# A hybrid decoder step on one core: the decode tail reordered, the output weights loaded inside it, and the gate rows sent through memory

## The reference, cut to what matters

```python
    mod = jax.nn.silu(c) @ lp['w_ada'] + lp['b_ada']
    shift, scale, gate = jnp.split(mod, 3, axis=-1)
    ...
    mixed = jnp.concatenate([jax.nn.silu(mla_gate) * o_mla,
                             jax.nn.silu(rw_gate) * o_rw,
                             jax.nn.silu(gm_gate) * o_gm], axis=-1)
    out = jnp.einsum('ble,ed->bld', mixed, lp['w_out'])
    y = x + gate[:, None] * rms_norm(out, lp['norm_post_g'])
```

## Time and profile before

| | us |
|---|---|
| median of three runs | 1983.21 (1981.27 to 1985.27) |
| the profiled execution | 1974.86 |
| its span, first to last instruction | 1973.3 |
| TensorE busy | 1854.2 |
| DVE busy | 899.1 |
| ACT busy | 514.2 |
| the last block of layer 0 begins | 854.8 |
| the last block of layer 1 begins | 1831.4 |

### The profile page before, as it was taken

How to read it: one execution, slowest core, us unless ns; L and a number is a source line. 1 busy time by engine, 2 the same in 40 slices (tenths; PEclk the granted TensorE clock), 3 DMA queues, 4 the chain that set the end, 5 groups by cost and what they waited for, 6 DMA issues and landing times. The chain is left out here.

```text
span 1973.3 us, 45874 instructions
## 1 busy us (share of the span) xinstructions
PE 1854.2 (94%) x19360; PEld 1160.5 (59%) x19360; DVE 899.1 (46%) x2001; ACT 514.2 (26%) x1186; POOL 181.3 (9%) x175
## 2 busy tenths in 40 slices
PE   3999999999998999989969999999999979998998
PEld 2565676666665666654436656766566646666543
DVE  2124133232585777745230430432318677776542
ACT  3111022222422343411221111222224124343212
POOL 0010000002333100000000200000202340000000
PEclk9999999999999999979989999999999999998899
DMA  9600001000114766353064001010001166662531
GB/s 388 226 11 28 22 22 33 22 11 22 36 54 133 215 195 186 117 215 139 33 238 166 1 27 33 11 33 22 22 23 51 38 183 202 191 191 67 216 139 44
DMA packets 104503, 197.47 MB, mean 100 GB/s; under 512 B 17226, under 2 KB 87324, under 8 KB 100068
## 3 DMA queue, kind: packets, MB, share of 16 engines
q1 hardware_dynamic: 104292, 194.48, 29.8%
HBM read 181.70 MB, written 21.19 MB: 103 GB/s over the span
## 5 line engine op out<-in xcount | busy, mean ns | idle before, releaser
L825 PE MATMUL PB<-RB,R 128*128 128x344 f32 x1632 | 493.2, 455 | 0.0
L825 PEld LDWEIGHTS PB<-RB,R 128*128 128x128 f32 x1632 | 302.0, 190 | 156.4 <-issue 15.2
L2023 PE MATMUL PB<-RB,R 128*128 128x512 f32 x512 | 221.2, 592 | 0.0
L1651 PE MATMUL PB<-WUQ,Q 32*32 32x256 f32 x5120 | 198.8, 385 | 15.8 <-DVE WUQ L1812 9.5
L1812 DVE STREAM_TRANSPOSE WUQ<-RB 128x512 f32<-128x512 f32 x316 | 203.1, 679 | 14.2 <-DMA RB<-in_cache 11.5
L2023 PEld LDWEIGHTS PB<-RB,R 128*128 128x128 f32 x512 | 97.0, 190 | 120.8 <-issue 118.6
L985 ACT ACTIVATE R<-PB 128x344 f32<-128x344 f32 x90 | 41.2, 458 | 401.9 <-PE PB L825 401.9
L1240 DVE TENSOR_TENSOR PB<-PB,CST 128x128 f32<-128x128 f32 x64 | 18.8, 294 | 222.0 <-PE PB L845 222.0
L1651 PEld LDWEIGHTS PB<-WUQ,Q 32*32 32x32 f32 x5120 | 89.4, 104 | 41.3 <-issue 24.6
L673 PE MATMUL PB<-RB,R 128*128 128x344 f32 x288 | 85.4, 459 | 1.8 <-PEq L250 1.8
L1122 DVE COPY R<-PB 128x320 f32<-128x320 f32 x16 | 7.9, 492 | 146.7 <-PE PB L684 146.7
(11 more groups left out here) (368 smaller groups left out, 2658.6 us busy)
## 6 DMA issues: line engine op xcount, KB each, us to landing
RB<-in_cache SPq DMA_DIRECT2D x512, 160.0 KB, 2.6
R<-in_w_in SPq DMA_DIRECT2D x44, 512.0 KB, 3.7
R<-in_w_ada SPq DMA_DIRECT2D x14, 1536.0 KB, 12.5
RB<-in_w_ada SPq DMA_DIRECT2D x6, 1536.0 KB, 13.3
RB<-in_w_out SPq DMA_DIRECT2D x8, 1024.0 KB, 10.4
RB<-out_x_stream SPq DMA_DIRECT2D x2, 4096.0 KB
out_x_stream<-RB SPq DMA_DIRECT2D x16, 512.0 KB
RB<-in_x_prompt SPq DMA_DIRECT2D x1, 4096.0 KB
```

The source lines that it names most:

```text
L825: mm = pe.matmul(jobbank(j)[:, 0:CH], ring[:, blkno[n] % 4, k, :], hT[:, k, chunk(c)], start=(k == 0), stop=(k == KT - 1))
L1651: mm = pe.matmul(PB[qp[o], 2 * (h % 2) + q % 2, 0:256], Q4[qp[q], g, :], k[qp[q], c], start=(g == 0), stop=(g == NB - 1), skip_group_check ...
L2023: mm = pe.matmul(PB[0:n, 2 * (t % 2) + hf, :], mixT[:, k, cols(t)], wo[:, k, hf * 512:(hf + 1) * 512], start=(k == 0), stop=(k == 5))
```

## The change

The w_out loads move into the decode block, behind the last page loads, as their buffers come free; so do the loads of the decode rows and of w_uv. The tail gets a new order with new words: `WP(k)` is tile 0's projection for one k (k=0, 1, 2), and `GT` turns `gp` into rows on TensorE, which ACT copies out and SP writes to memory in four pieces. The last block reads them back, the prompt's row spread over 128 partitions by the DMA. `PV` is now four words of eight records. A square root of one element is put behind GT on ACT. In the last block tile 0's k=3 and half of tile 1 stand between the units of the normalisation, and the load of `ada[1]` joins the three others. The diff, cut:

```diff
+            gp = sm2[:, 80:152].rearrange("p (k c) -> p k c", c=9)
+            wuv2 = R4[:, 2066:3090].rearrange("p (r c) -> p r c", r=2)
+            grows = R4[:, t6 + 624:t6 + 880]
+            gate_rows = a["scr"].rearrange("v b c -> (v b) c")[NS:NS + 36].rearrange("(r g) c -> r g c", g=4)
...
-            TAIL = [(NH - 1, "PT", 0), (NS, "rw", "Z0"), (NH - 1, "PV", 0), (0, "FC", 1), (NS, "rw", "U0"), (0, "FC", 2), (NS, "rw", "H0"),
-                    (NS, "rw", "G0"), (0, "FC", 3), (NS, "rw", "Z1"), (0, "FC", 4), (NS, "rw", "U1"), (0, "FC", 5), (NS, "rw", "H1"),
-                    (0, "FC", 6), (NS, "rw", "OO")]
+            PE_PLAN = PE_PLAN[:-1] + rec("Z0") + PE_PLAN[-1:] + [wp(0)] + rec("U0") + [(NH - 1, "PT", 0)] + rec("H0") + [fc(1), wp(1)] + \
+                rec("Z1") + [fc(2), pv(0)] + rec("U1") + [pv(1)] + rec("H1") + [pv(2), pv(3), fc(4)] + rec("OO") + [wp(2), fc(6), (0, "GT", 0)]
+            ACT_PLAN = ACT_PLAN[:-2] + rec("Z0") + ACT_PLAN[-2:] + rec("U0") + [(NH - 1, "PT", 0)] + rec("Z1") + [fc(3)] + rec("U1", "OO") + [(0, "GT", 0)]
+            DVE_PLAN = pair_plan(DVE_PAIR) + [fc(1)] + rec("H0", "G0") + [fc(2), fc(3), fc(4)] + rec("H1") + [fc(5), fc(6)]
...
                     sp.dma_start(a["scr"][0].rearrange("b (m c) -> (b m) c", c=16), svo).then_inc(sv_io, 16)
+                    sp.wait_ge(sv_io, 16 * 10)
+                    sp.dma_start(orow, a["scr"][0]).then_inc(s_or, 16)
+                    sp.wait_ge(pg_free, 28)
+                    for i in (0, 1):
+                        sp.dma_start(wo[:, 2 * i:2 * i + 2], dram("w_out")[:, 2 * i:2 * i + 2]).then_inc(s_wo[i], 16)
+                    sp.wait_ge(pg_free, 30)
+                    for i in (3, 2):
+                        sp.dma_start(wo[:, 2 * i:2 * i + 2], dram("w_out")[:, 2 * i:2 * i + 2]).then_inc(s_wo[i], 16)
+                    sp.wait_ge(ta_done, NS)
+                    sp.wait_ge(ak_done, NS)
+                    sp.dma_start(wuv2, dram("w_uv")).then_inc(s_uv, 16)
                     sp.wait_ge(st_done, NCH + 1)
                     sp.dma_start(dram("wkv_p"), S0[:, NCH % 4]).then_inc(sv_io, 16)
-                    sp.wait_ge(sv_io, 16 * 11)
+                    sp.wait_ge(gr_done, 1)
+                    for g in range(4):
+                        sp.dma_start(gate_rows[:, g], grows[32 * g:32 * g + 9]).then_inc(sv_io, 16)
+                    sp.wait_ge(sv_io, 16 * 15)
...
+                        elif what == "WP":
+                            pe.wait_ge(xe_done, NH - 1)
+                            pe.wait_ge(s_wo[g // 2], 32)
+                            for hf in range(2):
+                                pe.matmul(PB[:, hf, :], mixT[:, g, 0:P], wo[:, g, hf * 512:(hf + 1) * 512], start=(g == 0), stop=False)
+                        elif what == "GT":
+                            pe.wait_ge(st_done, 1)
+                            pe.wait_ge(ty_done, NS)
+                            for k in range(KT):
+                                mm = pe.matmul(PB[32 * (k // 2):32 * (k // 2) + 9, 5, (k % 2) * P:(k % 2 + 1) * P], gp[:, k, :], ident, start=True, stop=True, skip_group_check=True)
+                            mm.then_inc(gr_full, 1)
...
+                        elif what == "GT":
+                            act.wait_ge(gr_full, 1)
+                            act.activation(grows, PB[:, 5, 0:256], ACT.Identity).then_inc(gr_done, 1)
+                            act.activation(sm2[:, 152:153], ones[:, 0:1], ACT.Sqrt)
...
+                    rows9 = a["scr"].rearrange("v b c -> (v b c)").rearrange("(r c) -> r c", c=D)[2:11]
+                    sp.dma_start(gg, rows9[0:1].broadcast_to([P, D])).then_inc(s_gate, 16)
+                    sp.dma_start(gs, rows9[1:9]).then_inc(s_gate, 16)
...
                     mean(0)
                     mean(1)
+                    project(0, [3])
                     var(0)
                     var(1)
                     mean(2)
                     mean(3)
...
+                    project(0, [6, 7])
                     var(2)
+                    project(1, [0, 1, 2, 3])
+                    project(0, [4, 5])
                     var(3)
                     mean(4)
                     mean(5)
-                    project(0, [4, 5])
+                    project(1, [6, 7, 4, 5])
                     var(4)
                     var(5)
-                    for t in ORD[1:]:
+                    for t in ORD[2:]:
```

More of the change, by code:

```diff
@@ L1667, in _ @@
                             f = h % 2
[L1668 to L1675, removed]
-                                pe.drain().then_inc(ol_full, 1)
+                            s, q = g, 2 * h + g // 2
+                            for c in range(4):
+                                mm = pe.matmul(PB[qp[c], 7, f * KVL:(f + 1) * KVL], PT[:, s, 32 * c:32 * c + 32], qpage(q)[:, (4 * s + c) % 8, RP:RP + KVL],
+                                               start=(h == 0 and s == 0), stop=(h >= NH - 2 and s == 3), skip_group_check=True)
+                            if s % 2 == 1:
+                                mm.then_inc(pg_free, 1)
+                            if h == NH - 1 and s == 3:
+                                pe.drain().then_inc(ol_full, 1)
+                        elif what == "WP":
[9 more added lines that the diff above has]
+                            mm.then_inc(gr_full, 1)
                         elif what == "FC":
@@ L1977, in _ @@
                 def _(sp):
-                    sp.dma_start(wuv2, dram("w_uv")).then_inc(s_uv, 16)
-                    sp.dma_start(orow, a["scr"][0]).then_inc(s_or, 16)
-                    for i in (0, 1, 3, 2):
-                        sp.dma_start(wo[:, 2 * i:2 * i + 2], dram("w_out")[:, 2 * i:2 * i + 2]).then_inc(s_wo[i], 16)
+                    rows9 = a["scr"].rearrange("v b c -> (v b c)").rearrange("(r c) -> r c", c=D)[2:11]
+                    sp.dma_start(gg, rows9[0:1].broadcast_to([P, D])).then_inc(s_gate, 16)
+                    sp.dma_start(gs, rows9[1:9]).then_inc(s_gate, 16)
                     sp.dma_start(xt[:, 0:NT, :], a["x_stream"][lay, 0:S].rearrange("l (t p) d -> p (l t) d", p=P)).then_inc(s_x, 16)
                     sp.dma_start(xt[0:NS, NT, :], a["x_stream"][lay, S:T].rearrange("l p d -> (l p) d")).then_inc(s_x, 16)
-                    sp.dma_start(ada[1], following(1)).then_inc(pf_in, 16)
                     for t in ORD:
@@ L2014, in project @@
                         n = rows(t)
-                        if ks[0] == 0 and t >= 2:
+                        if t == 1 and ks[0] == 0:
+                            pe.wait_ge(om_done, 1)
+                        if t >= 2 and ks[0] == 0:
                             pe.wait_ge(ot_done, t - 1)
@@ L2049, in _ @@
                     mean(3)
-                    pe.wait_ge(dg_done, 1)
-                    project(0, [0, 1, 2, 3, 6, 7])
+                    pe.wait_ge(s_or, 16)
+                    for f in range(2):
+                        pe.transpose(PB[:, 3, f * NS:(f + 1) * NS], orow[:, f * P:(f + 1) * P], ident[0:NS, 0:NS])
+                    pe.wait_ge(s_uv, 16)
+                    for h in range(H):
+                        for r in range(2):
+                            mm = pe.matmul(PB[:, 2, h * NS:(h + 1) * NS], wuv2[:, r, h * P:(h + 1) * P], olat[:, r, h, :], start=(r == 0), stop=(r == 1))
+                    mm.then_inc(om_full, 1)
+                    project(0, [6, 7])
                     var(2)
+                    project(1, [0, 1, 2, 3])
+                    project(0, [4, 5])
                     var(3)
```

78 lines of the change are left out of this document (31 added, 47 removed).

## The result

The changed kernel takes 1990.74 us (median of 20 runs, 1982.65 to 1997.25); the kernel before, beside it on the same chip, 1983.41 (20 runs, 1976.11 to 1991.67). The ratio is 1.0037, 95% interval 1.0023 to 1.0051: 7.3 us slower. I had forecast 1977.5, 5.7 us faster, in a range of 1968 to 1990, and the time lies just above it. The profiled execution after took 1993.13 us with a span of 1991.5; the one before was a low one of its kernel (1974.86), so I compare stretches and leave the two spans aside.

A forecast was written before the change was run, and what follows sets the result against it. The time was taken to be decided between the last decode pair and output tile 2, where TensorE is not dense and partly at 1.2 GHz. Gains of 3.1 us (layer 1) and 2.6 (layer 0) sum to 5.7: 1977.5, range 1968 to 1990.

The forecast's parts named there:

- Loads: w_out's 4 MB in pair 7, x rows and the ada[1] prefetch: nothing waits; zero for all, bounds 0 and +1 us.
- The tail: Decode tail, layer 1: full clock, 12.6 us sum, gate rows through memory uncovered; next block begins at 1833.0, 1.6 later.
- The last block: From its start T, after 3.9 us of TensorE idle: DVE arrives last, tile 2 starts at T+39.5.
- the stall: Before tile 2 in the last block: TensorE idle 6.4 us until DVE's read of tile 0's bank in leave(0).
- the clock's return: Last block: 4 us at half clock from its start; 2.0 us lost to low clock once tile 2 starts.
- The slower one: Clock falls in the decode tail: 13.6 us of low clock make it 6.8 longer; 1991.1 us; chance 0.15.
- The one with the slow returns of the clock: Last block: both clock returns take twice as long, 3.6 us a layer, 7.2 against 5.7; 1984.7, no change; chance 0.25.
- The one without a stall: Last block: DVE's chain is shorter, tile 2 starts at T+33.1 at full clock; 22.5 us gained, 1960.7; chance 0.08.

The follow-up runs named there:

- the execution with the early variances: Changed kernel with var 2, var 3, mean 4, mean 5 before tile 1's first four k and var 4, var 5 before its last four: 1965.43 us, ratio 0.9938.
- the thin kernel: Changed kernel with its w_out loads cut to 64 of 1024 columns each, same DMAs, waits and places: 1965.66 us, ratio 0.9948 to the kernel before.
- the 512 KB kernel: Changed kernel with variances moved earlier and w_out in eight DMAs of 512 KB, four issued at once per burst: 1964.14 us, ratio 0.9950.
- the copy kernel: Kernel before, plus two 2 MB memory-to-memory copies in the middle of each layer's decode, SP waiting for each: 1998.53 us, ratio 1.0088.

## Why the prediction was wrong

**The step that failed** is "Loads": "the queues stand at 4 GB/s there, so nothing waits. ... Zero for all of these, bounds 0 and +1 us." I asked who waits for the loads, and found nobody. I did not ask what else uses the DMA engines while they move. The page names it in its third part, an "instruction" queue beside the data's, and the trace of before had its traces: idle times marked `issue` of 1.1 to 1.4 us during page loads, one of which I had before me (the idle time near 780.5). An instruction packet passes at 779.0 to 779.5 there, 2 us ahead of TensorE's start at 781.44. The term's size is 5.3 us in layer 0 and 7.3 in layer 1, 12.6 against a bound of 1 (10.1 if the execution with the early variances stands for the changed kernel's pair 7). The row that I cited for the 4 GB/s also belongs to the tail: in pair 7 itself the trace of before has 198 GB/s from 1780 to 1790 and 3 from 1800 to 1810.

**The tail** I had too long. In the thin kernel the stretch from the copies of TB (end 1803.9) to the block takes 20.1 us; before it took 20.5 (1831.4 less 1810.9), and I had 22.1. The gate rows' 16 records take 0.64 us, not 1.9, the idle time before the block 3.34 and not 3.9, and in this kernel the clock stayed up, as forecast: 0.98 from 1803 on. Layer 0's stretch takes 20.2 us where it took 20.0. This is 1.4 us in layer 0 and 2.0 in layer 1 in the change's favour against my sum. The Trainium skill, page "DMA: Bandwidth & Descriptors", section "Anatomy of one DMA — SWDGE (gpsimd) path", gives about 2 us of fixed cost for a DMA that GpSimd issues. SyncE issues these, so that I had carried the figure over to another path; it would have made this wait longer, and the trace went the other way: the last of the four writes is issued at about 1852.1 and the block begins 1.8 us later, its end included.

**The last block** held in layer 1, step by step: finish(0) at T+7.4 (forecast 7.7), DVE's wait for var 3 6.71 us (6), variance(4) at T+34.7 (34.9), tile 2 at T+39.35 (39.5), the stall 6.15 (6.4), no second stall. What did not hold is the clock's return, for which I had one figure. Ten microseconds from the block's start and from the stall's end, layer 0 and then layer 1:

```profile
868.18:878.18 10.00, 10.00 (x33) 5.96 (x33) 4.29 (x7) 2.94 (x6) 0.00 (x0) 0.71 0.86 323
908.85:918.85 10.00, 10.00 (x17) 4.30 (x18) 9.36 (x11) 2.15 (x4) 0.00 (x0) 0.70 0.13 52
...
1853.88:1863.88 10.00, 10.00 (x37) 6.36 (x38) 5.54 (x8) 2.94 (x6) 0.00 (x0) 0.85 0.85 324
1893.23:1903.23 10.00, 10.00 (x18) 4.44 (x19) 9.36 (x11) 2.15 (x4) 0.00 (x0) 0.77 0.13 54
```

A mean of 0.71 over 10 us costs 2.9 us. So the return at the block's start cost 2.9 us in layer 0 and 1.5 in layer 1 (2.0 forecast), the one behind the stall 3.0 and 2.3 (2.0). The block as a whole is 4.3 us shorter than before in layer 1, where my terms gave 4.7 (5.1 less 2.0, plus the 1.6 later start), and 2.3 in layer 0, where they gave 4.2. In the thin kernel it is 3.8 shorter in layer 0 and 2.1 in layer 1 (139.8 us to the span's end), so the difference goes with the execution and not with the layer.

**The sum with measured sizes.** Tails +0.2 and -0.4 (from the thin kernel) and blocks -2.3 and -4.3 give -6.8. The bursts add 10.1 to 12.6: +3.3 to +5.8, where +7.3 (4.6 to 10.1) was measured. The thin kernel's own parts, -0.2, -3.8 and -2.1, give -6.1, where -10.3 (6.9 to 13.7) was measured. Some 4 us of the thin kernel's gain are left over; I found no place for them in single profiles, whose page waits differ by more, and they stay open.

**The rivals.** The slower one (tail at half clock) gave 1991.1, almost the measured time, by a mechanism that the trace refutes: the low spells, one of them in the tail (1833 to 1837), stand behind the idle times of the bursts, 4 us each, and vanish without them. The near number is luck. (By its own terms the gain would be used up at 5.7 us of low clock a layer and not 5.4, and 4 us slower would be reached at 9.7 and not 9.4.) The one with the slow returns of the clock came in part in layer 0, where they took 1.9 us more than in my sum; alone it led to no change, 1984.7. The one without a stall did not come.

## What to carry to other kernels

Before moving a bulk load under compute, ask what else passes through the DMA engines, TensorE's own instructions first: a stream of many small products eats a 16 KB packet every 4 us, and 2 MB queued at once hold the next one up. Issue such a load in portions (here 1 MB or less under way at a time), and look at what stands behind the waits on the issuing queue: with one 256 KB piece in flight they cost here as much as they saved. An idle time marked `issue` in the middle of a group, with the DMA share near 1 ahead of it, is the sign; where a chain of another engine (here var 3 for DVE) is the last arrival, put its input first, even ahead of work that is ready.

## What the runs showed of the hardware that I had not expected

- TensorE's instructions come in packets of about 16 KB through the same DMA engines as data. In four bursts of the changed kernel, in the 512 KB kernel and in the copy kernel TensorE started 2 to 2.9 us after the late packet passed. That the packets of q8 are TensorE's is inferred from their count (154 for 38,700 records), these times and the fixed number of records ahead of each stop (8700 and 9083 in layer 0, with the gate rows' records ahead of it or behind); who asks for them, and when, no run shows.
- 2 MB in the queue made idle times of 0.9 to 4.2 us; 1 MB at a time 0.97 at most. Idle times of 0.9 to 1.0 us marked `issue` stay even with thin loads.
- The clock does not fall behind each of these idle times: 1.95 us idle in layer 0 left it at 1.00 (847.5 to 852.0), and 1.95 us in layer 1 brought it to 0.57 (1833 to 1837). The returns in the last block took from 3.0 us (10 us at a mean of 0.85) to 6.0 (0.70), worked out from the two levels.
- Products with 9 columns of weights and 128 columns of data, eight in all into four column groups, took 0.64 us for 16 records, 0.04 a record; I had scaled them by their columns and taken three times as long.
